# Banded attention at the end of a layer stack: scores issued behind the transposes, the minimum of a tile ahead of the scaling of the one before it, and the gate's tanh and product moved to tiles 2 and 3

## What is computed

```python
def sliding_window_attention(q, k, v, sinks, slopes):
    # blocks of 128 queries; keys of the block and of the one before it
    logits = jnp.einsum('bnqkgd,bnskd->bnkgqs', qb, kk).astype(jnp.float32) * scale
    logits = logits - sl * dist.astype(jnp.float32)
    logits = jnp.where(valid[None, :, None, None], logits, -jnp.inf)
    p = jax.nn.softmax(jnp.concatenate([logits, sink], axis=-1), axis=-1)[..., :-1]
    return jnp.einsum('bnkgqs,bnskd->bnqkgd', p.astype(v.dtype), vv)

def odd_layer(h, w_in, b_in, sinks, w_out):
    q, k, v, g = jnp.split(h @ w_in + b_in, ODD_SPLITS, axis=-1)
    o = sliding_window_attention(q, k, v, sinks, alibi_slopes(SW_HEADS))
    return (o * jax.nn.silu(g)) @ w_out
```

## Time and profile before

| | us |
|---|---|
| median of 3 runs | 2469.41 |
| lowest and highest | 2464.82, 2470.40 |
| the profiled execution, device time | 2468.76 |
| its span in the profile | 2466.9 |
| PE busy in the span | 2368.4 (96%) |
| DVE busy | 1493.0 (61%) |
| ACT busy | 1220.0 (49%) |
| mean granted TensorE clock | 0.989 |

### The profile page before, as it was taken

The page is one execution under the profiler, slowest core; times in us unless marked ns, Lnnn a source line. Parts: engine busy times, 40 slices in busy tenths (PEclk is TensorE's granted clock), DMA queues, the critical chain, the costliest instruction groups (busy, mean ns, idle before and its releaser), DMA issues. The chain is left out here.

```text
span 2466.9 us, 31321 instructions
## 1 busy us (share of the span) xinstructions
PE 2368.4 (96%) x11991; PEld 1953.2 (79%) x11991; DVE 1493.0 (61%) x2739; ACT 1220.0 (49%) x2205; POOL 185.2 (8%) x112
## 2 busy tenths in 40 slices
PE   7999899998999999999999999999999999999988
PEld 6777687887888777788888887888787787888776
DVE  6767756536656657655555555653476665666665
ACT  5545633224545544666666555332455434656552
POOL 0000021000000043000000000000112030000022
PEclk9999999999999999999999999999999999999999
DMA  3222422112221332111110111224434431111143
GB/s 130 81 73 81 137 92 75 66 66 81 89 89 53 112 106 69 49 39 43 35 43 26 43 35 35 85 102 177 170 127 159 137 94 55 35 52 45 47 136 120
DMA packets 93135, 203.05 MB, mean 82 GB/s; under 512 B 10368, under 2 KB 45568, under 8 KB 91968
## 3 DMA queue, kind: packets, MB, share of 16 engines
q1 hardware_dynamic: 92992, 201.12, 24.3%
HBM read 160.13 MB, written 40.96 MB: 82 GB/s over the span
## 5 line engine op out<-in xcount | busy, mean ns | idle before, releaser
L224 PE MATMUL acc<-operand_hi,w_hi 128*128 128x512 f32 (+1 forms) x1814 | 733.3, 404 | 31.9 <-DVE operand_lo L370 9.5
L226 PE MATMUL acc<-operand_hi,w_lo 128*128 128x512 f32 (+1 forms) x1814 | 711.1, 392 | 0.0
L225 PE MATMUL acc<-operand_lo,w_hi 128*128 128x512 f32 (+1 forms) x1814 | 709.9, 391 | 0.0
L224 PEld LDWEIGHTS acc<-operand_hi,w_hi 128*128 128x128 f32 x1814 | 343.5, 189 | 109.2 <-issue 22.3
L226 PEld LDWEIGHTS acc<-operand_hi,w_lo 128*128 128x128 f32 x1814 | 343.1, 189 | 74.2
L225 PEld LDWEIGHTS acc<-operand_lo,w_hi 128*128 128x128 f32 x1814 | 344.0, 190 | 67.1 <-issue 3.3
L192 DVE TENSOR_TENSOR w_lo<-w_raw,w_hi 128x1024 fp32r<-128x1024 f32 (+2 forms) x203 | 228.3, 1125 | 175.3 <-ACT w_hi L186 173.0
L186 ACT ACTIVATE w_hi<-w_raw 128x1024 fp32r<-128x1024 f32 (+2 forms) x203 | 197.2, 972 | 277.1 <-PE aux L226 141.9
L224 PE MATMUL aux<-operand_hi,w_hi 128*128 128x512 f32 x618 | 250.1, 405 | 20.6 <-DVE resid L3238 5.0
L226 PE MATMUL aux<-operand_hi,w_lo 128*128 128x512 f32 x618 | 242.6, 393 | 0.0
L225 PE MATMUL aux<-operand_lo,w_hi 128*128 128x512 f32 x618 | 242.1, 392 | 0.0
(11 more groups left out here) (463 smaller groups left out, 3848.4 us busy)
## 6 DMA issues: line engine op xcount, KB each, us to landing
w_raw<-in_stream SPq DMA_DIRECT2D x201, 512.0 KB, 3.6
ssd_e<-cs_scratch SPq DMA_DIRECT2D x8, 1024.0 KB, 6.8
g_scratch<-ssd_work SPq DMA_DIRECT2D x12, 512.0 KB, 2.9
ssd_xbc<-g_scratch SPq DMA_DIRECT2D x8, 768.0 KB, 4.9
y_scratch<-rnn_y SPq DMA_DIRECT2D x10, 512.0 KB, 2.6
out_a_raw<-y_scratch SPq DMA_DIRECT2D x19, 256.0 KB, 4.4
resid<-in_x SPq DMA_DIRECT2D x8, 512.0 KB, 8.7
g_scratch<-mlai_g SPq DMA_DIRECT2D x8, 512.0 KB, 2.9
```

The source lines that it names most:

```text
L224: pe.matmul(out, w_hi, x_hi, start=first, stop=False)
L225: pe.matmul(out, w_hi, x_lo, start=False, stop=False)
L226: return pe.matmul(out, w_lo, x_hi, start=False, stop=last)
```

## The change

In slot n:

- PE issues the scores of n + 2 right behind the transposes of n, ahead of the projection. Tile 0 of the next pair is an exception (its scores stay at the end of slot 6, since its queries are ready late), and tile 1 of the next pair is scored behind the transposes of tile 7.
- DVE takes the minimum of n + 2 first, then the side work (now in `beside`), then the scaling of n + 1. In slot 6 it is the scaling of 7, the side work, then the minimum of the next pair's tile 0; in slot 7 it is the minimum of the next pair's tile 1, the side work, and the scaling of its tile 0.
- ACT does the exponentials of n + 2 behind the copy of n. The gate is cut in two: the Identity stays in slot 0, the Tanh goes to slot 2, and DVE's product to slot 3. The slopes go from slot 2 to slot 3.
- In the last pair DVE's `split_lo` of slot 0 stands ahead of the scaling of tile 1, `begun.low(n - 1)` takes the place of `begun.low(n)` in slot n and stands ahead of the scaling of n + 1.
- DVE's wait for the gate and for the stored y moves from slot 0 to the end of slot 3. Ahead of the loop one more minimum and one more group of exponentials are done.

No instruction with data is added or taken away; the same ones stand in another order.

```diff
@@ -3453,6 +3453,10 @@
                         mm = pe.transpose(turned[:, at:at + P], probs[:, n % 2, e, kt * P:(kt + 1) * P],
                                           k.ident[:, :])
                 mm.then_inc(s["pt"], 1)
+                if n + 2 < QT:
+                    pe_scores(pe, p, par, n + 2, None)
+                elif n + 1 == QT and not last:
+                    pe_scores(pe, p + 1, 1 - par, 1, nxt[0])
                 if not last:
                     t = nxt[n // 4]
                     if n % 4 == 0:
@@ -3471,10 +3475,8 @@
                     for m in range(n - GROUP + 1, n + 1):
                         mm = values_by_columns(pe, m)
                     mm.then_inc(s["pv"], 1)
-                if n + 2 < QT:
-                    pe_scores(pe, p, par, n + 2, None)
-                elif not last:
-                    pe_scores(pe, p + 1, 1 - par, n + 2 - QT, nxt[0])
+                if n + 2 == QT and not last:
+                    pe_scores(pe, p + 1, 1 - par, 0, nxt[0])
 
         pairs(pe, pair)
 
@@ -3505,6 +3507,8 @@
         act.wait_ge(k.tile_done[t.slot], t.before + 1)
         act.activation(g[:, :], k.acc[:, t.slot, :], ACT.Identity,
                        bias=k.vec[:, bass.ds(VEC["b_g"] + p, 1)]).then_inc(k.acc_free[t.slot], 1)
+
+    def act_tanh(act, t):
         act.wait_ge(k.acc_free[t.slot], t.before + 1)
         act.activation(tg[:, :], g[:, :], ACT.Tanh, scale=0.5).then_inc(s["tanh"], 1)
 
@@ -3528,6 +3532,7 @@
         act_queries(act, q_tile(0, 0), 0, 0, first_q)
         split_hi(act, k, Tile(j0, 4, per, 0))
         act_exp(act, 0, 0)
+        act_exp(act, 0, 1)
 
         def pair(i, par, last):
             p = 2 * i + par
@@ -3535,11 +3540,13 @@
                 N = QT * p + n
                 act.wait_ge(s["pt"], N + 1)
                 act.activation(pth[:, n % GROUP, :], turned, ACT.Copy).then_inc(s["pth"], 1)
-                if n + 1 < QT or not last:
-                    act_exp(act, p if n + 1 < QT else p + 1, (n + 1) % QT)
+                if n + 2 < QT or not last:
+                    act_exp(act, p if n + 2 < QT else p + 1, (n + 2) % QT)
                 if n == 0:
                     act.wait_ge(s["y"], groups * p)
                     act_gate(act, g_tile(i, par), p)
+                if n == 2:
+                    act_tanh(act, g_tile(i, par))
                 if last:
                     if n == 0:
                         act.wait_ge(k.tile_done[g_tile(i, par).slot], g_tile(i, par).before + 1)
@@ -3554,7 +3561,7 @@
                         split_hi(act, k, begun.tile(2))
                 if n in (1, 5) and not last:
                     split_hi(act, k, g_tile(i, par + 1) if n == 1 else q_tile(i, par + 2))
-                if n == 2 and not last:
+                if n == 3 and not last:
                     act_slopes(act, p + 1, 1 - par)
                 if n == 4 and not last:
                     act_queries(act, q_tile(i, par + 1), p + 1, 1 - par, k.acc[:, q_tile(i, par + 1).slot, :])
@@ -3619,39 +3626,48 @@
         split_lo(dve, k, Tile(j0, 4, per, 0))
         dve.wait_ge(s["sinks"], 1)
         dve_max(dve, 0, 0)
+        dve_max(dve, 0, 1)
         dve_norm(dve, 0, 0)
+
+        def beside(i, par, p, n, last):
+            if n in (2, 7) and not last:
+                split_lo(dve, k, g_tile(i, par + 1) if n == 2 else q_tile(i, par + 2))
+            if n in (5, 6) and not last:
+                dve_queries(dve, q_tile(i, par + 1), p + 1, 1 - par, n - 5,
+                            k.acc[:, q_tile(i, par + 1).slot, :])
+            if n == 3:
+                dve.wait_ge(s["tanh"], p + 1)
+                dve.scalar_tensor_tensor(out=g[:, :], in0=tg[:, :], scalar=1.0, in1=g[:, :],
+                                         op0=ALU.add, op1=ALU.mult).then_inc(s["gate"], 1)
+            if last and n == 0:
+                split_lo(dve, k, begun.tile(1))
+            if last and n:
+                begun.low(dve, n - 1)
 
         def pair(i, par, last):
             p = 2 * i + par
             for n in range(QT):
                 N = QT * p + n
-                more = n + 1 < QT or not last
-                after = (p if n + 1 < QT else p + 1, (n + 1) % QT)
-                if more:
-                    dve_max(dve, *after)
-                if n in (2, 7) and not last:
-                    split_lo(dve, k, g_tile(i, par + 1) if n == 2 else q_tile(i, par + 2))
-                if n in (5, 6) and not last:
-                    dve_queries(dve, q_tile(i, par + 1), p + 1, 1 - par, n - 5,
-                                k.acc[:, q_tile(i, par + 1).slot, :])
-                if more:
-                    dve_norm(dve, *after)
-                if n == 0:
-                    dve.wait_ge(s["tanh"], p + 1)
-                    dve.scalar_tensor_tensor(out=g[:, :], in0=tg[:, :], scalar=1.0, in1=g[:, :],
-                                             op0=ALU.add, op1=ALU.mult).then_inc(s["gate"], 1)
-                    dve.wait_ge(s["gate"], p + 1)
-                    dve.wait_ge(s["stored"], 16 * p)
-                if last:
-                    if n == 0:
-                        split_lo(dve, k, begun.tile(1))
-                    if n < SW_PAIRS - 1:
-                        begun.low(dve, n)
-                    if n == 6:
-                        begun.low(dve, SW_PAIRS - 1, y[:, 0:HALF])
-                    if n == 7:
-                        split_lo(dve, k, begun.tile(2))
+                if n + 2 < QT:
+                    dve_max(dve, p, n + 2)
+                elif n + 2 > QT and not last:
+                    dve_max(dve, p + 1, 1)
+                if n + 2 == QT:
+                    dve_norm(dve, p, n + 1)
+                beside(i, par, p, n, last)
+                if n + 2 == QT and not last:
+                    dve_max(dve, p + 1, 0)
+                if n + 2 < QT:
+                    dve_norm(dve, p, n + 1)
+                elif n + 2 > QT and not last:
+                    dve_norm(dve, p + 1, 0)
+                if last and n == QT - 1:
+                    begun.low(dve, SW_PAIRS - 1, y[:, 0:HALF])
+                    split_lo(dve, k, begun.tile(2))
                 if n % GROUP == GROUP - 1:
+                    if n < GROUP:
+                        dve.wait_ge(s["gate"], p + 1)
+                        dve.wait_ge(s["stored"], 16 * p)
                     dve.wait_ge(s["pv"], N // GROUP + 1)
                     at = slice((n + 1 - GROUP) * P, (n + 1) * P)
                     dve.scalar_tensor_tensor(out=y[:, at], in0=out_v, scalar=0.5, in1=g[:, at],
```

## The result

The changed kernel is slower: 2482.02 us (median of 6 runs, 2477.31 to 2483.33) against 2467.57 us for the kernel before (6 runs, 2463.46 to 2470.40), a ratio of 1.0051 with a 95% interval of 1.0042 to 1.0061, or 10 to 15 us. The forecast was 2479 us, with a range of 2472 to 2486.

A forecast was written before the change was run, and what follows sets the result against it. PE was taken to bound ordinary pairs, the chain over PE, ACT and DVE the last pair. 2468.76 + 3.3 (ordinary pairs) + 6.7 (last pair) = 2478.8, so about 2479 us, range 2472 to 2486.

The forecast's parts named there:

- the sum's 2478.8: Whole kernel: profiled time before, 2468.76 us, plus 3.3 us for ordinary pairs and 6.7 us for the last pair.
- The minimum at S + 1.12: DVE's minimum of n + 2 starts 1.12 us after the slot's start, waiting for scores; bounds 0.8 and 1.3.
- Slot 1 falls to the undisturbed length: Ordinary pairs: without the wait behind the gate, slot 1 drops from 4.85 to about 3.7 us.
- The gate's price of 1.12 us a pair: Ordinary pairs: the wait behind the gate's Tanh and product lengthens slot 1 by 1.12 us, which the change removes.
- Slot 2 at 4.34 and slot 5 at 4.65: Ordinary pairs: the split and the queries delay the scaling, putting these slots 0.61 and 0.92 us over 3.73.
- An ordinary pair +0.47, together +3.3 us: Each of seven ordinary pairs: -1.12 gate, +0.61 and +0.92 new waits, +0.06 slower start behind a wait.
- Slot 0 of the last pair, 7.1 us: DVE's half of the weight split, waiting for ACT, precedes tile 1's scaling; its transposes start at 7.1 instead of 3.4 us.
- My load that could bind: SP's loads wait for DVE's later splits and lows; costed at nothing, 1 to 3 us once if they bind.
- The last pair +6.7 us: Last pair takes 41.8 us against 35.11, from the later slot 1, waits for `begun.low` and half clock in slot 1.
- the clock rival: Last pair: clock stays down from slot 2 on, 8 us more, 2487 us in all; chance 0.08.
- Small queues: SP's loads, the store of y and the extra minimum before the first pair: costed at nothing, at most small one-off costs.
- The rule that I set against the change: Last pair: frequent short idles between matmul groups can make PE's clock swing; new slots would idle 2 us.

The follow-up runs named there:

- e4: Kernel before with only the gate's move: Tanh in slot 2, DVE's product and the slopes in slot 3; 2461.29 us, 0.9975 of the kernel before.
- e1: Changed kernel with DVE's side work behind the scaling in the seven ordinary pairs only; 2467.41 us, 1.0001 of the kernel before.
- e8: Changed kernel with one more 128x1024 DVE addition in slots 0 and 4 of ordinary pairs; 2491.63 us, 1.0097 of the kernel before.
- e5: Changed kernel with dummy matmuls in PE's idle stretches of the last pair, slots 0 to 5; 2477.18 us, 1.0032 of the kernel before.
- e3: Changed kernel with side work behind the scaling in all pairs and `begun.low(n)` in slot n of the last; 2459.51 us, 0.9960.
- e6: Changed kernel with DVE's order scaling, minimum, side work in all pairs, and `begun.low(n)` in slot n of the last; 2458.15 us, 0.9961.
- e2: Changed kernel with, in the last pair alone, side work behind the scaling and `begun.low(n)` in slot n; 2468.76 us, 1.0008 of the kernel before.
- e7: e6 with 18 dummy matmuls on PE in slot 1 of the last pair; 2459.57 us, 0.9962 of the kernel before.
- e10: e9 with the first four operand rows loaded a pair earlier and 18 dummy matmuls in the last pair; 2459.68 us, 0.9965 of the kernel before.
- e9: Changed kernel with DVE's scaling first, then in the last pair `begun.low(n - 1)`, then minimum, then side work; 2458.18 us, 0.9962.

## Why the prediction was right

The result lies in the range and 3 us above the forecast. The waits came where they were forecast, in both kinds of pairs; that the sum came so near is in part luck, since its errors do not have one sign. In the profiled execution, 3.1 us above the sum's 2478.8, the last pair took 3.1 us more than forecast and the seven ordinary pairs 0.9 less, and 1.05 us arose ahead of the pairs. By its steps:

- *The minimum at S + 1.12, taken from the one slot without a projection.* Measured 1.11 (2140.21 behind 2139.10). The bounds of 0.8 and 1.3 were not needed.
- *Slot 1 falls to the undisturbed length.* 3.68 for 4.85. The gate's price of 1.12 us a pair was a little low: e4, which moves the gate alone, measured 1.27.
- *Slot 2 at 4.34 and slot 5 at 4.65.* Measured 4.31 and 4.61, in all seven pairs. e1 showed the cause by taking it away, e8 by adding side work to two more slots.
- *An ordinary pair +0.47, together +3.3 us.* Measured 35.22 - 34.86 = +0.36, together +2.4. The terms were +0.59 and +0.88 for slots 2 and 5, -1.17 for slot 1 and +0.10 each for slots 0 and 4, which I had at nothing. Slots 3, 6 and 7 stayed covered and took 0.14 us less together.
- *Slot 0 of the last pair, 7.1 us.* Measured 7.06. The chain over ACT's split was read rightly: `split_lo` waited 2.60 us for ACT, with the scaling behind it. My load that could bind (cost put at nothing) did not decide: the first part came at 2353.87, where `begun.low`, behind the minimum, set it.
- *The last pair +6.7 us.* Measured +9.8. This is the term that was mis-sized, and it was mis-sized in the clock. Without the clock I had 7.1, 4.4, 4.38, 7.6, 4.38, 4.38, 2.5, 5.4; e5, which holds the clock up, measured 7.08, 4.42, 4.36, 7.48, 4.41, 4.36, 2.44, 5.18. The sums are 40.1 and 39.7. For the clock I had put 1.7 us, in slot 1 alone; it cost 44.89 - 39.73 = 5.2 us, in slots 1, 2, 3, 5 and 6. So the clock rival, which I gave 0.08 and priced at 8 us more (+14.7 in all, where my bound says +14), was partly true: about 3.5 us of it came.
- *Small queues.* SP's loads, the store of y and the additional minimum ahead of the first pair cost nothing that shows; the 1.05 us by which the first pair began later was there already at the transposes of the values, 12.8 us ahead of the pairs in both kernels (L3431, 2083.77 instead of 2082.72 us).

The rule that I set against the change also came true in part. In the last pair the granted clock fell from 1.00 to half three times: in the 5.93 us of idle, then at about 2365 us in the idle of 2.9 us, and at about 2379 us, 1 us behind one of only 1.8 us (the rows of the result above: 0.50, 0.59, 0.52). It did not fall each time: behind the idle of 1.79 us ahead of the part of slot 4 it stayed at 1.00. Before, it fell once. The Trainium skill, TensorE: Matmul & The Clock Gate, section "A second HAM failure mode: psum-queue depth-cycling", says that repeated short idles between groups of matmuls can make the clock swing. The trace agrees as to the swing; the idles here are waits for DVE, not the cycling through PSUM that the section names.

The Trainium skill, TensorE: Matmul & The Clock Gate, section "Architectural detail: the array is 16× 32×32, not 1× 128×128", says that ScalarE's and VectorE's queues are strictly first in, first out. The trace agrees, and the loss in the ordinary pairs is of this kind: the scaling itself waited for nothing in 56 of 56 turns, and PE's 14 waits for it stood in the slots where a split or a query was ahead of it.

What the change was worth part by part, then: the gate's move -1.27 us a pair (e4); the scores two tiles ahead nothing more in an ordinary pair (33.55 to 33.69 us in e1, e3 and e6 against 33.60 in e4, since PE has no wait left to lose); the side work between a late minimum and the scaling +1.53 us a pair (e1); the order in the last pair +11.4 us (e2). Of the changed kernel's last pair 5.2 us are the clock (e5); how much of the 11.4 that is stays open, since e2's pair also ran at 0.90.

## What to carry to other kernels

When a step is moved ahead in an in-order queue, ask when its input comes: if it waits, everything behind it waits too, and work that was hidden before is then paid for as far as it stands over the bounding engine's own work, although its engine is idle for a third of the time. Put side work behind both the step that the bounding engine waits for and the step that has to wait for that engine's new output. Which of these two comes first mattered less here: the scaling first gave 0.14 us in an ordinary pair (33.55 for 33.69) and cost 0.9 in the last one (34.73 for 33.81), and the timed runs show no difference. Read the last iteration of a loop by itself: here, with one eighth of the pairs, it had four fifths of the pairs' loss (9.8 of 12.2 us).

## What the runs showed that I had not expected

- The clock is a second price of an idle PE, and not a fixed one. The last pair has the same code in the changed kernel, in e1 and in e8, and took 44.89, 44.91 and 47.15 us at granted clocks of 0.81, 0.81 and 0.75. Dummy matmuls bought back 5.16 us in the changed kernel (e5), 1.2 us in one slot and next to nothing in the pair in e7, and 1.5 us in e10.
- Stages that no run touched moved the start of the first pair between 2091.3 us (e1) and 2097.3 us (e10), a difference of 6.0 us, nearly half of the effect. The differences of 0.1% between medians could only be read as differences of pairs in the trace; the timed ratios agree with these sums within their intervals (e4: 7 x -1.27 + 0.44 = -8.5 us, 0.9966, timed 0.9975 [0.9965, 0.9985]).
- With three orders of the last pair in five runs (e3; e6 and e7; e9 and e10) it took between 33.8 and 36.0 us, although PE was busy for no more than 25.7 us of it without dummies: each order that removed one wait met the next chain over DVE and ACT. Which order would reach below 33 us stays open.
